# A hybrid decoder step on one core: ten places where the order of work around TensorE is changed

## What is computed

```python
h = _rmsnorm(x, p['norm_mix_w'])
a_v, a_g, b_u, c_z, c_xbc, c_dt = jnp.split(h @ p['w_in'], IN_SPLITS, axis=-1)
ya, conv_a_buf = _conformer_conv(a_v, a_g, ...)   # width 31, layer norm, silu
yb, s5_re, s5_im = _s5(b_u, ...)                  # complex recurrence, 32 groups x 64 states
yc, conv_c_buf, ssd_state = _mamba2(c_z, c_xbc, c_dt, ...)   # chunked SSD, 16 heads
x = x + jnp.concatenate([ya, yb, yc], axis=-1) @ p['w_out']
x = x + _cross_attention(_rmsnorm(x, p['norm_xa_w']), mem_k, mem_v, p['xa_wq'], p['xa_wo'])
f, ffn_buf = _conv_ffn(_rmsnorm(x, p['norm_ffn_w']), ffn_buf, ...)   # 2048 -> 5504 -> 2048
x = x + f
```

## Time and profile before

| | |
|---|---|
| median of three runs | 1818.94 us |
| the profiled execution, its time and its span | 1822.08 us, 1820.4 us |
| TensorE busy | 1794.2 us, 99% |
| VectorE, ACT, POOL busy | 62%, 40%, 14% |
| the chain that ended last | TensorE 89%, VectorE 2%, DMA 1%, ACT 1% |
| mean granted clock of TensorE | 0.997 |
| DMA | 316.47 MB, mean 174 GB/s |

### The profile page before, as it was taken

The page is one execution under the profiler, slowest core; times in us unless marked ns, Lnnn a source line. Parts: engine busy times, 40 slices in busy tenths (PEclk is TensorE's granted clock), DMA queues, the critical chain, the costliest instruction groups (busy, mean ns, idle before and its releaser), DMA issues.

```text
span 1820.4 us, 32709 instructions
## 1 busy us (share of the span) xinstructions
PE 1794.2 (99%) x12542; PEld 1642.9 (90%) x12542; DVE 1131.2 (62%) x1968; ACT 730.2 (40%) x1102; POOL 251.7 (14%) x267
## 2 busy tenths in 40 slices
PE   9999999999999999999999999999999999999998
PEld 7877789777778999966999999999999999999998
DVE  6998977788776464443356555655555566446544
ACT  3101366344454343343234444444433445444444
POOL 1024200033321230000131000000000000003200
PEclk9999999999999999999999999999999999999999
DMA  8333544556667585486455555555555556555552
GB/s 253 105 116 105 186 127 149 162 184 209 190 186 245 165 281 187 131 343 268 145 166 160 166 163 163 167 165 161 163 165 167 162 152 180 163 165 160 172 161 98
DMA packets 157956, 316.47 MB, mean 174 GB/s; under 512 B 16938, under 2 KB 39482, under 8 KB 152931
## 3 DMA queue, kind: packets, MB, share of 16 engines
q1 hardware_dynamic: 153525, 307.73, 54.2%
q10 hardware_dynamic: 4344, 7.56, 1.3%
HBM read 300.78 MB, written 14.89 MB: 173 GB/s over the span
## 4 chain that ended last, share of the span: by engine, by line
PE 89%; DVE 2%; DMA 1%; ACT 1%; issue 0%; SPq 0%; DVEq 0%; ACTq 0%
PE bank L872 22%; PE bank L874 21%; PE bank L873 21%; PE bank L835 17%; PE bank L1435 2%; PE bank L1447 1%; DMA raw<-in_w_out 1%; DMA raw<-in_xa_wo 1%; PE bank L1457 1%; PE bank L1280 0%; PE bank L1246 0%; PE bank L921 0%; PE bank L939 0%; DVE xlo L2385 0%; DVE raw_lo L2616 0%
## 5 line engine op out<-in xcount | busy, mean ns | idle before, releaser
L872 PE MATMUL bank<-hhi,whi 128*128 128x288 f32 x2128 | 631.8, 297 | 3.2 <-DVE hlo L2954 1.5
L873 PE MATMUL bank<-hlo,whi 128*128 128x288 f32 x2128 | 628.5, 295 | 0.0
L874 PE MATMUL bank<-hhi,wlo 128*128 128x288 f32 x2128 | 626.4, 294 | 0.0
L2851 DVE TENSOR_TENSOR wlo<-raw,whi 128x1024 fp32r<-128x1024 f32 (+1 forms) x270 | 330.8, 1226 | 378.2 <-ACT whi L1897 377.6
L1897 ACT ACTIVATE whi<-raw 128x1024 fp32r<-128x1024 f32 (+1 forms) x270 | 283.3, 1049 | 511.5 <-PE bank L874 503.4
L872 PEld LDWEIGHTS bank<-hhi,whi 128*128 128x128 f32 x2128 | 399.4, 188 | 4.5 <-issue 1.7
L874 PEld LDWEIGHTS bank<-hhi,wlo 128*128 128x128 f32 x2128 | 401.5, 189 | 0.0
L873 PEld LDWEIGHTS bank<-hlo,whi 128*128 128x128 f32 x2128 | 400.2, 188 | 0.1
L835 PE MATMUL bank<-hT,raw 128*128 128x288 f32 x768 | 191.1, 408 | 1.1 <-ACT xbr_a L1707 1.1
L835 PEld LDWEIGHTS bank<-hT,raw 128*128 128x128 f32 x768 | 144.4, 190 | 42.9 <-issue 4.3
L1831 ACT ACTIVATE khi<-raw 128x1024 fp32r<-128x1024 f32 x66 | 69.9, 1059 | 116.0 <-PE bank L835 113.6
(11 more groups left out here) (530 smaller groups left out, 2606.9 us busy)
## 6 DMA issues: line engine op xcount, KB each, us to landing
raw<-in_ffn_w_down SPq DMA_DIRECT2D x86, 512.0 KB, 3.8
raw<-in_ffn_w_gate SPq DMA_DIRECT2D x80, 512.0 KB, 3.7
raw<-in_ffn_w_up SPq DMA_DIRECT2D x80, 512.0 KB, 3.6
raw<-in_w_in SPq DMA_DIRECT2D x64, 512.0 KB, 3.7
raw<-in_xa_wk SPq DMA_DIRECT2D x32, 512.0 KB, 4.0
raw<-in_xa_wv SPq DMA_DIRECT2D x32, 512.0 KB, 4.1
raw<-in_w_out SPq DMA_DIRECT2D x32, 512.0 KB, 3.8
raw<-in_xa_wq SPq DMA_DIRECT2D x32, 512.0 KB, 3.9
```

The source lines that it names most:

```text
L872: pe.matmul(out, lhsT=wh[:, wo:wo + P], rhs=xh, start=first, stop=False)
L873: pe.matmul(out, lhsT=wh[:, wo:wo + P], rhs=xl, start=False, stop=False)
L874: return pe.matmul(out, lhsT=wl[:, wo:wo + P], rhs=xh, start=False, stop=last)
L2851: tt(wlo[:, s % 2, wsl], raw[:, s % 4, wsl], whi[:, s % 2, wsl].bitcast(F32), ALU.subtract)\
```

## The change

It reorders work at ten places and leaves the computation as it is. (1) S5 pairs go by the table S5_IN, outputs five slabs later. (2) The conformer's gated rows move into VectorE's scan loop, at j = 10 to 13. (3) `cat_b_high(0)`, `(1)` go from x = 54 to 53, `in_evac(6)` behind `cat_b_high(2)`, `(3)`; `gate_lo` and four `conv_c` steps one slab later. (4) On VectorE, `chunk_state(1)` goes from y = 7 to 8, `final_state` from 8 to 10 (on TensorE from 8 to 9), the terms three slabs and the sample tokens one slab later; two late taps at y = 11 go to 33 and 40. (5) `ssd_update(1)` and `(5)` go from y = 23 and 47 to 24 and 48, where they stand behind `ssd_a(2)` and `(6)`. (6) A 1 x 1 exponential after `cat_a_hi` at y = 53 brings ACT's table load there. (7) W_out's banks are awaited one by one, and all `gate_scale`s stand behind `k_split(65)`. (8) `x_back` is issued after split 3 of W_out instead of split 5. (9) `p_values(6)` goes behind the sample's values and `p_values(7)` into bank 6 as a whole, behind `osum`'s transposes; split 1 of W_o goes behind `osum`; W_o's slabs wait for `o_lo` in two steps. (10) The `fx` transposes start without the last `act`, and the down projection's first slab takes the eight banks in the order in which `fx` is done with them (FX_BANK) instead of waiting for all eleven rounds.

The diff, without the lists of semaphore names and the lines that only pass `o_bank(n)` (bank 4 for n < 7, else bank 6) and FX_BANK to ACT and VectorE:

```diff
@@ -346,6 +346,7 @@
 FLOOP = FT - 2
+FX_BANK = (0, 1, 2, 3, 7, 4, 5, 6)
@@ -405,7 +409,7 @@
-S5_AT = 17
+S5_IN = (17, 20, 22, 25, 27, 30, 32, 34)
 BUS_AT = 10
@@ -413,19 +417,19 @@
 N_SPLIT = NA - SPLIT_AT
-LATE_TAPS = {11: 2, 13: 2, 14: 2, 15: 1, 16: 1, 19: 2, 20: 2, 21: 1, 22: 1, 25: 2, 26: 2, 27: 1, 28: 1,
-             31: 1, 32: 2, 33: 1, 34: 1, 37: 2, 38: 2, 39: 1}
+LATE_TAPS = {13: 2, 14: 2, 15: 1, 16: 1, 19: 2, 20: 2, 21: 1, 22: 1, 25: 2, 26: 2, 27: 1, 28: 1,
+             31: 1, 32: 2, 33: 2, 34: 1, 37: 2, 38: 2, 39: 1, 40: 1}
 CONF_AT = 44
...
 TOKENS_AT, STATES_AT, CB_AT, SSD_AT, SSD_HALF, SSD_STEP, GATE_AT = 1, 6, 9, 12, 3, 6, 60
-TERMS_AT = 7
+TERMS_AT = 10
 K_TURN_AT = (10, 17, 29, 35)
...
 N_IN_K = 3
-PV_AFTER = {3: (0,), 4: (1, 2), 5: (3, 4), 6: (5,), 7: (6,), 8: (7,)}
+PV_AFTER = {3: (0,), 4: (1, 2), 5: (3, 4), 6: (5,), 7: (6, 7)}
@@ -1066,9 +1070,9 @@
         for pair in range(SJ // 2):
-            if x == S5_AT + 5 * pair // 2:
+            if x == S5_IN[pair]:
                 s5_in(pair)
-            if x == S5_AT + 5 + 5 * pair // 2:
+            if x == S5_IN[pair] + 5:
                 s5_out(pair)
@@ -1306,7 +1310,7 @@
             chunk_state(y - STATES_AT)
-        if y == STATES_AT + 2:
+        if y == STATES_AT + 3:
             final_state()
@@ -1380,9 +1384,10 @@
     def before_out(m):
-        pe.wait_ge(*at("kv_read_a", 8))
-        pe.wait_ge(*at("kv_read_v", 8))
-        pe.wait_ge(*at("gate_read", 2))
+        if m < 2:
+            pe.wait_ge(*at(("kv_read_a", "kv_read_v")[m], 8))
+        else:
+            pe.wait_ge(*at("gate_read", 2))
     four_groups(G_OUT, before_out, "x_out", ready_cat)
@@ -1406,19 +1411,18 @@
-    def p_values(n, part=range(4)):
+    def p_values(n):
...
         pe.wait_ge(*at("pT", n + 1))
-        if n >= 1:
+        if 1 <= n < 7:
             pe.wait_ge(*at("o_lo", n))
-        for d in part:
+        for d in range(4):
             for t in range(MT):
                 c0 = (4 * h + d) * P
-                q = mm(B[4][:, d * P:(d + 1) * P], vtok[:, t, c0:c0 + P], pT[:, n % 2, t, :],
+                q = mm(o_bank(n)[:, d * P:(d + 1) * P], vtok[:, t, c0:c0 + P], pT[:, n % 2, t, :],
                        t == 0, t == MT - 1)
-        if 3 in part:
-            q.then_inc(S("pv"), 1)
+        q.then_inc(S("pv"), 1)
@@ -1476,10 +1480,10 @@
             p_turn(n)
-    for n in range(N_IN_K, 8 + 1):
+    for n in range(N_IN_K, 8):
         if n < 7:
             scores(n + 1)
-        if n < 8:
+        if n < 7:
             p_values(n - 1)
@@ -1493,21 +1497,25 @@
             sample_values(b)
-    p_values(7, (0, 1))
+    p_values(6)
     pe.wait_ge(*at("osum", 1))
...
     x.then_inc(S("os_t"), 1)
-    p_values(7, (2, 3))
+    p_values(7)
...
     def ready_o(k):
-        pe.wait_ge(*at("os_lo", 1))
-        pe.wait_ge(*at("o_lo", 8))
+        if k == 0:
+            pe.wait_ge(*at("o_lo", 6))
+            pe.wait_ge(*at("os_lo", 1))
+        if k == 12:
+            pe.wait_ge(*at("o_lo", 8))
     def ff_columns(s):
...
         pe.wait_ge(*at("ff_rows", 16 * 4))
+        pe.wait_ge(*at("o_lo", 8))
         for i in range(2):
@@ -1517,7 +1525,7 @@
             q.then_inc(S("ff_t"), 1)
-    four_groups(G_O, never, "x_o", lambda k: ready_o(k) if k == 0 else None, ff_columns)
+    four_groups(G_O, never, "x_o", ready_o, ff_columns)
@@ -1533,16 +1541,20 @@
-    pe.wait_ge(*at("act", FT))
     for r in range(11):
+        pe.wait_ge(*at("taps", min(4 * r + 4, FT)))
+        if r == 0:
+            pe.wait_ge(*at("g_read", FT))
+            pe.wait_ge(*at("act", 4 * FPAIRS))
+        if r == 5:
+            pe.wait_ge(*at("act", FT))
         if r >= 8:
...
         for t in range(4 * r, min(4 * r + 4, FT)):
-            q = pe.transpose(B[r % 8][0:18, (t % 4) * P:(t % 4 + 1) * P], gcol[:, t, :], ident[:, :])
+            q = pe.transpose(B[FX_BANK[r % 8]][0:18, (t % 4) * P:(t % 4 + 1) * P], gcol[:, t, :], ident[:, :])
         q.then_inc(S("fx_t"), 1)
...
-    pe.wait_ge(*at("fx_read", 11))
     for half in range(2):
@@ -1557,7 +1569,12 @@
             split_in(f)
-            for m in range(DG):
+            for i in range(DG):
+                m = i
+                if first and half == 0:
+                    r = (i + 3) % DG
+                    m = FX_BANK[r]
+                    pe.wait_ge(*at("fx_read", r + 9 if r < 3 else r + 1))
                 if first and half == 1:
@@ -1851,16 +1868,16 @@
             mem_rows(1, 0, D // 2)
+            cat_b_high(0)
+            cat_b_high(1)
         if x == 54:
             mem_rows(1, D // 2, D)
-            cat_b_high(0)
-            cat_b_high(1)
             s5_tanh(2)
...
         if x == 55:
-            in_evac(6)
             cat_b_high(2)
             cat_b_high(3)
+            in_evac(6)
         if x == 56:
@@ -1952,7 +1969,7 @@
             a(cs2[NS:NS + NH, :], cs_rest[0:NH, :], ACT.Copy).then_inc(S("cs_terms"), 1)
-        if y == STATES_AT + 3:
+        if y == STATES_AT + 5:
             sc_.wait_ge(*at("st_out", 1))
@@ -1979,6 +1996,7 @@
                 a(hhi[:, t, :], va[:, t, :], ACT.Copy).then_inc(S("cat_a_hi"), 1)
+            a(xsum[0:1, 1, 0:1], ident[0:1, 0:1], ACT.Exp)
         if y == GATE_AT + 1:
@@ -2024,6 +2042,7 @@
     split(G_OUT, 3)
+    sc_.dma_start(xT[:, :, :], x_spill).then_inc(S("x_back"), 16)
     wait_used_B(sc_, G_OUT, 1)
@@ -2032,7 +2051,6 @@
     split(G_OUT, 5)
-    sc_.dma_start(xT[:, :, :], x_spill).then_inc(S("x_back"), 16)
     split(G_OUT, 6)
@@ -2095,16 +2113,17 @@
                 a(dst, src, ACT.Copy).then_inc(S("pTm_a"), 1)
-        if n < 8:
+        if n < 7:
             o_hi(n - 1)
...
     split(G_O, 0)
-    split(G_O, 1)
     sc_.wait_ge(*at("pv_sample", NB))
...
       B[5][:, :].rearrange("p (d h t) -> p h d t", d=4, h=XH), ACT.Copy).then_inc(S("os_hi"), 1)
+    split(G_O, 1)
+    o_hi(6)
     o_hi(7)
@@ -2459,6 +2478,15 @@
+    def glu_a(tiles):
+
+        for t in tiles:
+            v.wait_ge(*at("in_read", 8 + t + 1))
+            stt(up[:, t, HA:UP], th[:, t, 0:NP], 1.0, va[:, t, 0:NP], ALU.add, ALU.mult)\
+                .then_inc(S("u_done"), 1)
+            stt(up_sample(t)[:, :, HA:US], vsplit(th[:, t, NP:T], NB), 1.0, vsplit(va[:, t, NP:T], NB),
+                ALU.add, ALU.mult).then_inc(S("u_done"), 1)
+
     def s5_turn_back(j):
@@ -2493,6 +2521,8 @@
             .then_inc(S("s5_scanned"), 1)
+        if j in (10, 11, 12, 13):
+            glu_a((j - 10,))
         if j == SJ - 1:
@@ -2506,12 +2536,6 @@
-    for t in range(4):
-        v.wait_ge(*at("in_read", 8 + t + 1))
-        stt(up[:, t, HA:UP], th[:, t, 0:NP], 1.0, va[:, t, 0:NP], ALU.add, ALU.mult)\
-            .then_inc(S("u_done"), 1)
-        stt(up_sample(t)[:, :, HA:US], vsplit(th[:, t, NP:T], NB), 1.0, vsplit(va[:, t, NP:T], NB),
-            ALU.add, ALU.mult).then_inc(S("u_done"), 1)
     def gate_lo(m):
@@ -2616,8 +2640,8 @@
-    conv_steps = {49: (0, 1), 50: (2, 3), 51: (4, 5), 52: (6, 7), 54: (8, 9), 56: (10, 11), 57: (12, 13),
-                  58: (14, 15), 59: (16, 17)}
+    conv_steps = {49: (0, 1), 50: (2, 3), 51: (4, 5), 52: (6, 7), 53: (8,), 54: (9,), 55: (10,), 56: (11,),
+                  57: (12, 13), 58: (14, 15), 59: (16, 17)}
     for x in range(SPLIT_AT + 1, NA):
@@ -2631,8 +2655,9 @@
             gated(x - 52)
+        if x in (54, 56):
+            gate_lo(x - 54)
             gate_lo(x - 53)
-            gate_lo(x - 52)
         if x >= 62:
@@ -2781,13 +2806,13 @@
             token_rows(y - TOKENS_AT - 2)
-        if y in (STATES_AT, STATES_AT + 1):
-            chunk_state(y - STATES_AT)
-        if y == STATES_AT + 2:
+        if y in (STATES_AT, STATES_AT + 2):
+            chunk_state((y - STATES_AT) // 2)
+        if y == STATES_AT + 4:
             final_state()
...
             c_b()
-        if y == CB_AT + 1:
+        if y == CB_AT + 2:
             sample_tokens()
@@ -2806,6 +2831,10 @@
             ssd_c(j)
+            if y % 8 != 7:
+                ssd_update(j)
+        j = ssd_at(y, SSD_AT + SSD_HALF + 3)
+        if j is not None and y % 8 == 0:
             ssd_update(j)
@@ -2838,11 +2867,8 @@
             gate_root(y - GATE_AT - 1)
-        if y == NKV - 1:
-            for j in range(4):
-                gate_scale(j)
     k_split(NKV + 1)
-    for j in range(4, YT):
+    for j in range(YT):
         gate_scale(j)
@@ -2987,15 +3013,16 @@
                 v.tensor_copy(dst, src).then_inc(S("pTm_v"), 1)
-        if n < 8:
+        if n < 7:
             o_lo(n - 1)
     split(G_O, 0)
-    split(G_O, 1)
     v.wait_ge(*at("os_hi", 1))
...
         .then_inc(S("os_lo"), 1)
+    split(G_O, 1)
+    o_lo(6)
     o_lo(7)
```

(12 more changed lines are left out.)

## The result

The changed kernel is slower: 1829.35 us, median of four runs (1828.76 to 1831.65), against 1819.15 for the kernel before (four runs, 1818.72 to 1820.35). The ratio is 1.0057 (95% interval 1.0045 to 1.0069), 10 us. The forecast of 1820.9 and its range to 1826.0 missed it. The profiled execution of the changed kernel has a span of 1827.0 us against 1820.4, so 6.6 us of the difference can be followed step by step. Of the rest, 2.9 us are the profiled execution of before, which lay that much above its runs' median (1822.08 us), and 0.6 us that of the changed kernel, which was the shortest of its four (1828.76 us).

What follows compares the result with a forecast made beforehand. The prediction took TensorE, busy 99% of the span, as the bound, through its pauses and low-clock stretches. Its terms for the places and the clock summed to +2.0 us on 1818.94, giving 1820.9 us, range 1811.0 to 1826.0.

Steps and rivals of the forecast that it cites:

- places 1 and 2: Recurrence pairs and gates: the loop's end is held by the table, so the conv_a taps gain almost nothing, -0.3 us.
- place 3: Gate halves and in_evac(6): slab 56 waits for zs behind VectorE's gated rows, a pause of nearly 5 us, +3.0 us.
- place 4: Chunk states: the 2.2 us pause and the half clock behind it go, 1 us stays at k_turn(0), -2.5 us.
- place 5: State updates: s transposes at y=24 and y=48 wait 2.27 us each, a 0.6 us pause goes, +3.9 us.
- place 6: Table load brought ahead at y=53, before khi and raw_lo are late: -1.2 us.
- place 7: First W_out banks awaited singly, four gate scales no longer before raw_lo(65): -0.9 us.
- place 8: Residual's earlier read: the 1.4 us xT pause goes, W_out slab 5 waits 2.5 us for its weights, +1.0 us.
- place 9: Last values: the osum and hlo pauses go, about 1.1 us is left at the last softmax, -1.7 us.
- clock: TensorE's clock falls once behind the five new pauses of 2 us or more: +1.7 us (0 to +8.5).
- Rival A: New waits at slab 56 and the s transposes do not come, nor the clock's fall: 1810.3 us, chance 0.23.
- rival C: Residual's early read starves W_out's loads more than once, +3.7 instead of +1.0: 1823.6 us, chance 0.05.
- Rival B: TensorE's clock falls after all five new pauses, 8.5 us instead of 1.7: 1827.7 us, chance 0.20.

Runs made afterwards that it cites:

- the four undone edits: Changed kernel with S5 pairs 3 and 5 back, in_evac(6) first, updates right behind ssd_c, residual's read behind split 5: 1809.37 us, ratio 0.9953.

## Why the prediction was wrong

It was a forecast of no change; the sum of +2.0 should have been about +10. Term by term, from the table of steps:

| | predicted | in the two profiles |
|---|---|---|
| places 1 and 2 | -0.3 | +1.7 |
| place 3 | +3.0 | +3.5 |
| place 4 | -2.5 | -3.3 |
| place 5 | +3.9 | +3.8 |
| place 6 | -1.2 | -1.3 |
| place 7 | -0.9 | -1.1, then +0.5 at slab 2 |
| place 8 | +1.0 | +4.6 - 1.5 = +3.1 |
| place 9 | -1.7 | -2.3 |
| place 10 | -1.0 | -1.0 |
| clock | +1.7 | +2.6 + 1.6 = +4.2 |

(Place 3: 5.18 - 1.68. Place 4: 4.53 - 7.81, its own half clock included. Place 5: 6.01 - 4.53 and 8.36 - 6.01. Place 8: 11.06 - 6.49 at slab 5 and 11.14 - 12.68 at Q. Clock: 7.81 - 5.18 and 12.68 - 11.06. Place 9: 8.82 - 11.14. Place 10: 6.59 - 7.53.) The column sums to 7.8; 1.3 go off for a half-clock stretch in W_o that the profile of before has and the changed kernel's has not (7.53 - 8.82), which gives 6.5 of the 6.6.

Right were places 3, 5, 6, 7 and 10 to half a us, and 4 and 9 to 0.8: the walks by durations of the trace of before held, and the waits foretold at slab 56, at both s transposes and at the last softmax came where they were placed. The pause foretold at slab 48 came too, behind a raw_lo that starts at 241.13 and ends 0.1 us ahead of TensorE's 242.45, but with 1.0 us and not 2. Rival A, that the new waits don't come, was wrong.

Three steps failed.

*Places 1 and 2.* The step was "the table holds it there: the last two pairs keep their slabs". The loop's end hangs on pair 5 as well: its output moved from slab 34 to 35, turn_back(12) waited for it until 190.95, the three turns behind it, with POOL's products, had no room to catch up, and the taps started at 209.29 instead of 207.27. Taking pairs 3 and 5 back undoes it. The bound of +0.5 was too narrow, because I looked at the last pairs and not at how long the chain behind the one before them is.

*Place 8.* The mechanism was named (rival C), its size was not. "I take 2.5" should have been 4.6. I took the 3.87 us that ACT had waited for slab 8 as the most that slab 5 could wait; in the event it was 7.15, and 4.3 at TensorE. In the kernel before, slab 8's load was issued 0.7 us ahead of the read (569.75 against 570.45), and by the bytes of queue 1 about half of it had got through when the read's first packet moved, nine tenths 1.6 us later (an estimate); here slab 5's load was issued 2.9 us behind the read (569.98 against 567.04), with most of the 512 KB of stores still ahead of it. A delay measured where the load is well under way is no upper bound for one where it has not begun. The early read alone and its undoing agree within their intervals (4.7 us lost, 4.2 won back), though alone it is slab 4 that waits.

*The clock.* "I count one fall" of 1.7 us. There were two, the first of them twice as long as the one I had taken as a measure. Rival B was right in its direction but not in its count: behind the waits of 2.3 us at y=24 and y=48 the changed kernel's profile shows no fall. Another execution, that of the kernel with the read put back, does. And two is the least: the profiled execution is the shortest of the four, with a mean granted clock of 0.996; two of the others have 0.994 and 0.993 (1829.81 and 1831.65 us), so more of their time ran at half clock. Where, no profile shows.

The rest, 3.5 us between the 6.7 by which the two profiled executions differ in time and the 10.2 of the runs, is for 2.9 us the profiled execution of before (1822.08 against a median of 1819.15). I had said so and then took for granted that differences carry over. The mean granted clock of every timed execution shows what they missed. The profile of before, with two half-clock stretches besides that at the end of the kernel, has 0.997, and that of the four undone edits, with none, 0.999. Of the 49 executions of before that were timed beside the experiments, 24 have 0.999 and a median of 1818.46 us, 13 have 0.998 and 1820.30, 6 have 0.997 and 1820.88, 4 have 0.996 and 1822.54; two more have 1.0. So most executions of before hold less half clock than the one that I read. The fall behind vtok, 1.7 us, from which the price of a fall and a part of place 4 were taken, can't be in all of them, and place 4 should win less in the runs than the 3.3 us of the table; alone it won 2.0, with an interval that reaches to 3.6. How often the clock falls there was not counted.

## What to carry to other kernels

A pause is taken away by ending the wait that ends last without making another one later: of ten places here six won (place 2 among them, once place 1 no longer held the loop up) and four, places 1, 3, 5 and 8, gave back more, and undoing part of the four gave 1809.4 us, better than either kernel. For every instruction that moves back, walk to the one that overwrites what it reads, or needs what it makes, with durations from the trace; where a step gates a loop that has no slack left, a slab earlier or later counts in full. A large read with long runs, set loose beside many short ones, took most of the bandwidth here while it lasted (1.62 of 1.93 MB in five us); cut it to the same size, or issue it when nothing urgent is in flight.

## What the runs showed of the hardware

The granted clock at the same pause is not the same from one execution to the next. Behind slab 56's pause of 4.8 to 5.0 us it was low in each of the six profiles that had it, for about six us in five of them and about half as long in one; behind pauses of 2.2 to 2.3 us it was low in some profiles and not in others. It also fell in W_o without a pause of that length, in six of the thirteen profiles: the stretch of 850 to 895 us has a mean of 1.00 in the kernel of the four undone edits, and of 0.92 in the one that only moves gate_lo besides, whose W_o is the same. Such a fall costs 1.3 us and more, so single executions here differ by that much without a cause in the order of work.
